# Norm sums as columns per block of tokens, and the norm of the renewed x by recursion, in a two-layer diffusion backbone

## The chip, the cores and the metric

The kernel runs on one core of one Trainium2 chip. The metric is the device time of one launch in microseconds. The kernel before takes 2223.82 us, the median of 3 runs (2221.72 to 2227.89).

## The reference, cut to what matters

384 tokens (128 of context, 256 latent) of width 1024 go through two layers, all in float32. Each layer has three sub-layers: a gated feed-forward net of width 2816, a token mixer (two kinds of attention and a recurrence, joined and projected by `w_out`), and a second feed-forward net. Each is wrapped alike:

```python
h = modulate(x, norm_pre, shift, scale)      # rmsnorm(x) * g * (1 + scale) + shift
y = sublayer(h)
x = x + gate * rmsnorm(y, norm_post)         # gate halved around the feed-forward nets
```

`rmsnorm` divides each token by the root of the mean of its 1024 squares plus 1e-6. `shift`, `scale` and `gate` come from a product of the conditioning vector with `ada_w`, one set for the context tokens and one for the latent ones. The outputs are x at the end and the new caches.

## The kernel before

x, y and h lie transposed: a tile k is 128 of the 1024 features on the partitions by 384 tokens along the row, eight tiles in all. Float32 products are made of three passes: a weight is split into `w_hi` (ScalarE, L1037) and `w_lo` (GpSimd, L534, two pieces of 128x512), h into `h_hi` and `h_lo`, and each k-tile of a unit takes three products per 128 columns (L597). A unit is up to four k-tiles by 256 columns, 24 products, and four units are in flight (`SPLIT`). The raw weights come through a ring of four buffers, in the order that SyncE issues. Phases follow one another: up0, down0, proj with the mixer, out, up1, down1. The phases down0, out and down1 make y, in four pairs of tiles. A pair is 22 k-tiles deep after the feed-forward nets (five units of four k-tiles and one of two) and 8 deep in out (two units).

Between a phase that makes y and the next one lies a gap; there are five. In a y phase, ScalarE squares each pair of y out of PSUM (`y_square`, L1134) and VectorE multiplies it by the gate factors `mG` into `y` (`y_out`, L1605) and adds the squares up in `y_sum`. In the gap TensorE sums over the partitions by products with a matrix of ones (`y_sums`, L700), so that the sum stands in all 128 partitions; ScalarE takes the root of the 128x384 sums (L1097), VectorE its reciprocal, and adds y times the root to x (`post`, L1566). Then the same for x: ScalarE squares it (L1119), TensorE sums (`x_sums`, L710), root, reciprocal, and `pre` (L1531) scales x into `sq`, from which ScalarE makes `h_hi` (L1126) and VectorE `h_lo` (`low`, L1524). The next phase starts by k-tiles (`by_tiles`, L667): two head units take k = 0 to 3 as each h tile comes, a third k = 4 to 7, and then the fourth, 96 products in all.

Products of the ada groups (`ada_unit`, L624; 8 units make one group of 1024 columns) fill the gaps: 22 units in four of them, 8 in layer 1's second. VectorE transposes and copies each group (`ada_take`, L1404). Every engine runs its own program in order, written out by hand, with semaphores between; a step on VectorE (L1395) waits for its own end before the next instruction.

## Time and profile before

| | |
|---|---|
| median of 3 runs | 2223.82 us |
| profiled execution | 2221.89 us |
| its span | 2220.1 us |
| TensorE busy | 2138.8 us (96%) |
| VectorE busy | 917.4 us (41%) |
| ScalarE busy | 903.5 us (41%) |
| GpSimd busy | 1241.3 us (56%) |
| DMA | 311.37 MB, mean 140 GB/s |

All times within the profile count from the span's start. PE is TensorE, PEld its weight loads, DVE VectorE, ACT ScalarE, POOL GpSimd, SP SyncE. A "q" behind an engine is its sequencer. Matmuls are pipelined: each is listed with its own duration, and the distance between starts is shorter. Of the shares, TensorE's is the one to follow; an engine at 41% can still be the one that all wait for inside a gap of 20 us.

### The profile page before, as it was taken

How to read it: one execution, taken by the hardware profiler on the slowest of the kernel's cores; microseconds unless marked ns; L12 is line 12 of the kernel's file. 1: busy time of each engine (PE TensorE's matmuls, PEld its weight loads, DVE VectorE, ACT ScalarE, POOL GpSimd, SP SyncE). 2: the span in 40 equal slices, each digit the busy share in tenths (PEclk: the TensorE clock that was granted, in tenths of full speed). 3: DMA queues.
4: the chain of work that ended last, by engine and by line, in shares of the span. 5: the costliest groups of instructions: out<-in, count | busy, mean ns of one | idle time of the engine just before them, and what ended most of it. 6: DMA issues, size and time to landing. Idle time of an engine off the chain costs nothing.

```text
span 2220.1 us, 32126 instructions
## 1 busy us (share of the span) xinstructions
PE 2138.8 (96%) x13212; PEld 2023.3 (91%) x13212; DVE 917.4 (41%) x1486; ACT 903.5 (41%) x1269; POOL 1241.3 (56%) x972
## 2 busy tenths in 40 slices
PE   6999999999898999999999999999999899899998
PEld 4999997988898988999979999799888899799997
DVE  5122116446766464121151221534576665622122
ACT  3222323256765534223243232324567646422332
POOL 2666654434478454666646665354435965366663
PEclk8999999999999999999999999999999999999999
DMA  7555674423232384445554446553322235244431
GB/s 283 150 174 171 226 260 149 126 86 88 72 89 87 112 286 124 124 143 168 194 178 124 147 125 226 194 152 88 87 78 77 86 114 172 70 139 124 124 124 66
DMA packets 306921, 311.37 MB, mean 140 GB/s; under 512 B 9923, under 2 KB 285655, under 8 KB 306775
## 3 DMA queue, kind: packets, MB, share of 16 engines
q1 hardware_dynamic: 299671, 303.55, 43.7%
q10 hardware_dynamic: 7104, 5.77, 0.8%
q8 instruction: 104, 1.70, 0.3%
q14 instruction: 42, 0.34, 0.0%
HBM read 305.35 MB, written 3.93 MB: 139 GB/s over the span
## 4 chain that ended last, share of the span: by engine, by line
PE 74%; DVE 12%; ACT 8%; POOL 3%; issue 2%; DMA 0%; SPq 0%; DVEq 0%; ACTq 0%
PE X L597 57%; PE S L597 6%; PE Ab L597 4%; POOL w_lo L534 1%; PE S L714 1%; ACT w_hi L1037 1%; POOL dec L562 1%; POOL dec L561 1%; PE X L775 1%; PE S L804 1%; ACT p L1190 1%; DVE mg_lo L1462 1%; PE X L857 1%; DVE gate_b L1473 1%; DVE root L1547 1%
## 5 line engine op out<-in xcount | busy, mean ns | idle before, releaser
L534 POOL TENSOR_TENSOR w_lo<-raw,w_hi 128x512 fp32r<-128x512 f32 (+1 forms) x872 | 1163.8, 1357 | 938.3 <-ACT w_hi L1037 928.8
L1037 ACT ACTIVATE w_hi<-raw 128x1024 fp32r<-128x1024 f32 (+1 forms) x436 | 453.1, 1041 | 716.4 <-PE X L597 678.1
L597 PE MATMUL X<-h_hi,w_hi 128*128 128x384 f32 x1600 | 538.1, 336 | 13.2 <-DVE h_lo L1527 13.2
L597 PE MATMUL X<-h_lo,w_hi 128*128 128x384 f32 x1600 | 536.3, 335 | 0.0
L597 PE MATMUL X<-h_hi,w_lo 128*128 128x384 f32 x1600 | 536.1, 335 | 0.0
L597 PEld LDWEIGHTS X<-h_hi,w_hi 128*128 128x128 f32 x1600 | 301.6, 189 | 21.0 <-DVE h_lo L1527 16.5
L597 PEld LDWEIGHTS X<-h_hi,w_lo 128*128 128x128 f32 x1600 | 301.8, 189 | 0.0
L597 PEld LDWEIGHTS X<-h_lo,w_hi 128*128 128x128 f32 x1600 | 301.7, 189 | 0.0
L1599 DVE TENSOR_TENSOR prod<-X,silu 128x768 f32<-128x768 f32 x44 | 42.1, 957 | 561.5 <-PE X L597 561.5
L597 PE MATMUL X<-act_hi,w_hi 128*128 128x384 f32 x704 | 235.7, 335 | 0.0
L597 PE MATMUL X<-act_hi,w_lo 128*128 128x384 f32 x704 | 235.2, 334 | 0.0
L597 PE MATMUL X<-act_lo,w_hi 128*128 128x384 f32 x704 | 235.2, 334 | 0.0
L1610 DVE TENSOR_SCALAR y<-X,mG 128x128 f32<-128x128 f32 x96 | 33.4, 411 | 337.7 <-ACT prod L1141 337.7
L597 PE MATMUL S<-h_hi,w_hi 128*128 128x384 f32 x480 | 166.3, 346 | 0.4 <-DVE proj L1441 0.4
L597 PE MATMUL S<-h_lo,w_hi 128*128 128x384 f32 x480 | 161.3, 336 | 0.0
L597 PE MATMUL S<-h_hi,w_lo 128*128 128x384 f32 x480 | 161.3, 336 | 0.0
L597 PEld LDWEIGHTS X<-act_hi,w_hi 128*128 128x128 f32 x704 | 132.1, 188 | 2.1 <-issue 2.1
L597 PEld LDWEIGHTS X<-act_lo,w_hi 128*128 128x128 f32 x704 | 132.2, 188 | 0.0
L597 PEld LDWEIGHTS X<-act_hi,w_lo 128*128 128x128 f32 x704 | 132.1, 188 | 0.0
L597 PE MATMUL Ab<-h_hi,w_hi 128*128 128x384 f32 x320 | 111.7, 349 | 0.7 <-DVE acc_e L1449 0.7
L597 PE MATMUL Ab<-h_hi,w_lo 128*128 128x384 f32 x320 | 107.2, 335 | 0.0
L597 PE MATMUL Ab<-h_lo,w_hi 128*128 128x384 f32 x320 | 107.2, 335 | 0.0
(364 smaller groups left out, 3074.8 us busy)
## 6 DMA issues: line engine op xcount, KB each, us to landing
raw<-in_w_in SPq DMA_DIRECT2D x124, 512.0 KB, 3.8
raw<-in_ffn_gate SPq DMA_DIRECT2D x88, 512.0 KB, 3.8
raw<-in_ffn_up SPq DMA_DIRECT2D x88, 512.0 KB, 3.8
raw<-in_ffn_down SPq DMA_DIRECT2D x80, 512.0 KB, 3.5
raw<-in_ada_w SPq DMA_DIRECT2D x48, 512.0 KB, 3.7
hold<-in_ada_w SPq DMA_DIRECT2D x29, 512.0 KB, 5.1
first_w<-in_ada_w SPq DMA_DIRECT2D x16, 512.0 KB, 10.5
hold_a<-in_ada_w SPq DMA_DIRECT2D x16, 512.0 KB, 6.3
```

Of the source, the lines that this page charges most:

```text
L534: ins = nc.gpsimd.tensor_tensor(slot(w_lo, u)[:, part], raw_of(u)[:, part], slot(w_hi, u)[:, part], SUB)
L561: nc.gpsimd.tensor_tensor(dst[:, :, 0:b], mid, src[:, :, 0:b], SUB)
L562: nc.gpsimd.tensor_tensor(dst[:, :, b:], src[:, :, b:], mid, SUB).then_inc(S["dec_ready"], 1)
L597: mm = nc.tensor.matmul(dst, w[:, k, m * 128:m * 128 + 128], r_, start=start and k + j == 0, stop=stop and k == u.nk - 1 and j == 2)
L714: mm = nc.tensor.matmul(S5[:, 0:T], ones, sq[:, k, :], start=k == 0, stop=k == KT - 1)
L775: mm = nc.tensor.matmul(X[n % 2][:, c, at_:at_ + k.shape[-1]], proj[64 * c:64 * c + 64, (AQ if kind == "a" else CQ) + h, b * 128:b * 128 + ...
L804: mm = nc.tensor.matmul((S5, S6)[c][:, 0:128], v, pT[:, c, j * 128:j * 128 + 128], start=j == 0, stop=j == len(kbs) - 1)
L857: mm = nc.tensor.matmul(X[0][:, j // 3, j % 3 * 128:j % 3 * 128 + 128], lev_k[n % 2][:, t], lev_q[n % 2][:, t], start=True, stop=True)
L1037: A(slot(w_hi, u), raw_of(u), ACT.Copy).then_inc(hi_ready[u.split], 1)
L1190: e = A(p[n % 2][:, c, 0:w], X[n % 2][:, c, 0:w], ACT.Exp, bias=nmax[:, n % 2, c:c + 1], accum_out=esum[:, n % 2, c:c + 1])
L1599: V.tensor_tensor(prod[:, :, :], X[1][:, :, 0:T], silu[:, :, :], MUL).then_inc(x_free[1], 1)
L1610: ins = V.tensor_scalar(y[:, 2 * i + m, t0:t1], X[u.dest][:, m, t0:t1], mG[:, 2 * i + m, g:g + 1], None, MUL)
```

## The change

The norm sums are made as columns: `token_sums` multiplies each block of 128 tokens (as the stationary side) with a column of `pick`, and gives sums of 128 tokens by 3 blocks. Roots and reciprocals are then 128x3, and `spread` turns a column of reciprocals into 128x384 in PSUM by three transposes of the broadcast column (banks S6 and S5, `SPREAD`).

The sum of squares of the renewed x is not taken from x. With g = y times the gate factors and r the inverse root of y, it is the old sum plus 2 r sum(x g) + r^2 sum(g g), kept in `x_sum` (VectorE, in `joint`). The products x g are added on VectorE and g g is squared on ScalarE, during the y phase. `post` and `pre` become one function, `joint`, which renews x three tiles ahead of the one that it scales.

In the y phases ScalarE does the gating of y out of PSUM (`gated`), beside the squares, tile by tile; the last pair is taken up when its first tile is whole (`half_done`). VectorE adds squares and products up. The last w_hi of a y phase moves into `gap`, behind these. Factors for the next norm (`factors`) are made at the first y unit of out rather than at the last. TensorE's `gap` has ada units 0, 1, 2 to 5 and 6 to 21 between the sums. The ada groups use two banks in place of three. In the last y phase only the squares are summed.

Of the diff, its core (the rest renames semaphores, moves small buffers and merges GpSimd's list of low parts into one call):

```diff
-    prod, o = at("prod", [128, 2, T], f32, o)
+    prod, o = at("prod", [128, 4, T], f32, o)
...
-        MOD = [Ab, S7, S6]
+        MOD = [Ab, S7]
+        SPREAD = (S6[:, 0:T], S5[:, 0:T])
...
+            def tokens(rows):
+                return [rows[:, b * 128:b * 128 + 128] for b in range(NB)]
+            def token_sums(dst, rows, start, stop):
+                for b, r in enumerate(tokens(rows)):
+                    mm = nc.tensor.matmul(dst[:, 0:NB], r, pick[:, NB - 1 - b:2 * NB - 1 - b], start=start and b == 0,
+                                          stop=stop and b == NB - 1)
+                return mm
+            def spread(dst, col):
+                for b in range(NB):
+                    mm = nc.tensor.transpose(dst[:, b * 128:b * 128 + 128], col[:, b:b + 1].broadcast_to([128, 128]), ident)
+                mm.then_inc(S["spread_ready"], 1)
+            def y_sums():
+                pe.wait_ge(S["y_sq_ready"], seen.next("y_sq_ready", KT))
+                token_sums(S5, prod[:, 2, :], True, False)
+                pe.wait_ge(S["parts_ready"], seen.next("parts_ready"))
+                token_sums(S5, silu[:, 0, :], False, True).then_inc(S["sum_ready"], 1)
             def gap(units):
+                ada_unit(units[0])
                 y_sums()
-                early = 12 if len(units) > 12 else len(units) // 2
-                for u in units[:early]:
+                pe.wait_ge(x_free[0], seen.value(("xf", 0)) + 1)
+                token_sums(X[0][:, 0, 0:NB], y_sum, True, False)
+                ada_unit(units[1])
+                pe.wait_ge(S["r_ready"], seen.next("r_ready"))
+                spread(SPREAD[0], r_t)
+                token_sums(X[0][:, 1, 0:NB], silu[:, 1, :], True, False)
+                pe.wait_ge(S["parts_ready"], seen.next("parts_ready"))
+                token_sums(X[0][:, 0, 0:NB], part, False, True)
+                pe.wait_ge(S["c_made"], seen.next("c_made", KT))
+                token_sums(X[0][:, 1, 0:NB], prod[:, 3, :], False, True).then_inc(S["cross_ready"], 1)
+                for u in units[2:6]:
                     ada_unit(u)
-                x_sums([])
-                for u in units[early:]:
+                pe.wait_ge(S["r_ready"], seen.next("r_ready"))
+                spread(SPREAD[1], r_t)
+                for u in units[6:]:
                     ada_unit(u)
                 return by_tiles
...
             def x_sums(units):
...
-                    mm = nc.tensor.matmul(S5[:, 0:T], ones, sq[:, k, :], start=k == 0, stop=k == KT - 1)
+                    mm = token_sums(S5, sq[:, k, :], k == 0, k == KT - 1)
...
-            def root_of_sums():
-                act.wait_ge(S["sum_ready"], seen.next("sum_ready"))
-                A(root[:, :], S5[:, 0:T], ACT.Sqrt, bias=eps[:, 0:1], scale=1.0 / D).then_inc(S["root_ready"], 1)
-            def gap(units):
-                root_of_sums()
-                act.wait_ge(S["ada_used"], units[2].n + 1)
-                x_squares(0, KT)
-                root_of_sums()
+            def root_of_sums(sums):
+                A(r_q[:, :], sums, ACT.Sqrt, bias=eps[:, 0:1], scale=1.0 / D).then_inc(S["root_ready"], 1)
+            def gap(units, upto):
+                highs(upto)
+                act.wait_ge(S["x_sum_made"], seen.next("x_sum_made"))
+                root_of_sums(x_sum[:, :])
...
-            def y_square(u):
-                n = seen.next("y_pairs")
-                if n > 1:
-                    act.wait_ge(S["y_added"], n - 1 - (n - 1) // 4)
-                    act.wait_ge(S["sum_ready"], seen.value("sum_ready"))
-                A(prod[:, :, :], X[u.dest][:, :, 0:T], ACT.Square).then_inc(S["y_sq_ready"], 1)
+            def y_squares(halves_done, cross):
+                def squared(u, k):
+                    if k >= 3:
+                        act.wait_ge(S["y_added"], seen.next("y_added"))
+                    A(prod[:, k % 2 * 2, :] if k else silu[:, 0, :], X[u.dest][:, k % 2, 0:T], ACT.Square).then_inc(S["y_sq_ready"], 1)
+                def gated(u, k):
+                    for g, (t0, t1) in enumerate(((0, SEQ), (SEQ, T))):
+                        ins = A(y[:, k, t0:t1], X[u.dest][:, k % 2, t0:t1], ACT.Identity, scale=mG[:, k, g:g + 1])
+                    ins.then_inc(S["g_made"], 1)
+                    seen.next("g_made")
+                def gated_squared(k):
+                    if cross:
+                        act.wait_ge(S["g_made"], KT * seen.value("y_phases") + k + 1)
+                        A(prod[:, k % 2 * 2 + 1, :] if k else silu[:, 1, :], y[:, k, :], ACT.Square).then_inc(S["c_made"], 1)
+                def go(u):
+                    i = u.tag[1]
+                    if i < 3:
+                        act.wait_ge(unit_done[u.split], u.split_turn + 1)
+                        if i == 0:
+                            act.wait_ge(S["mg_factor_made"], seen.next("mg_factor_made"))
+                        for k in (2 * i, 2 * i + 1):
+                            squared(u, k)
+                            gated(u, k)
+                        return
+                    act.wait_ge(S["half_done"], halves_done)
+                    squared(u, 6)
+                    gated(u, 6)
+                    gated_squared(6)
+                    act.wait_ge(unit_done[u.split], u.split_turn + 1)
+                    squared(u, 7)
+                    gated(u, 7)
+                    act.wait_ge(S["sum_ready"], seen.next("sum_ready"))
+                    root_of_sums(S5[:, 0:NB])
+                    gated_squared(7)
+                    seen.next("y_phases")
+                def behind(u):
+                    if u.tag[1] < 3:
+                        for k in (2 * u.tag[1], 2 * u.tag[1] + 1):
+                            gated_squared(k)
+                return go, behind
...
+            def inverse_root():
+                dve.wait_ge(S["root_ready"], seen.next("root_ready"))
+                V.reciprocal(r_t[:, :], r_q[:, :]).then_inc(S["r_ready"], 1)
+                dve.wait_ge(S["r_ready"], seen.next("r_ready"))
...
+            def joint(units):
+                def add_to_x(k):
+                    step(V.tensor_tensor(y[:, k, :], y[:, k, :], SPREAD[0], MUL))
+                    step(V.tensor_tensor(x[:, k, :], x[:, k, :], y[:, k, :], ADD))
+                inverse_root()
+                dve.wait_ge(S["spread_ready"], seen.next("spread_ready"))
+                add_to_x(0)
+                dve.wait_ge(S["cross_ready"], seen.next("cross_ready"))
+                step(V.tensor_tensor(grown[:, :], X[0][:, 1, 0:NB], r_t[:, :], MUL))
+                step(V.scalar_tensor_tensor(grown[:, :], X[0][:, 0, 0:NB], 2.0, grown[:, :], MUL, ADD))
+                step(V.tensor_tensor(grown[:, :], grown[:, :], r_t[:, :], MUL))
+                step(V.scalar_tensor_tensor(grown[:, :], x_sum[:, :], -1.0, grown[:, :], MUL, ALU.max))
+                V.tensor_tensor(x_sum[:, :], x_sum[:, :], grown[:, :], ADD).then_inc(S["x_sum_made"], 1)
+                step(V.tensor_tensor(y[:, 1, :], y[:, 1, :], SPREAD[0], MUL))
+                inverse_root()
+                step(V.tensor_tensor(x[:, 1, :], x[:, 1, :], y[:, 1, :], ADD))
+                add_to_x(2)
+                dve.wait_ge(S["spread_ready"], seen.next("spread_ready"))
+                dve.wait_ge(S["ada_used"], units[2].n + 1)
+                for k in range(KT):
+                    for g, (t0, t1) in GROUPS:
+                        ins = V.scalar_tensor_tensor(sq[:, k, t0:t1], x[:, k, t0:t1], mA[:, k, g:g + 1], SPREAD[1][:, t0:t1], MUL, MUL)
+                    ins.then_inc(S["norm_ready"], 1)
+                    if k == 1:
+                        ada_take(units[7])
+                    if k:
+                        low(k - 1)
+                    if k + 3 < KT:
+                        add_to_x(k + 3)
+                    dve.wait_ge(S["norm_ready"], seen.next("my_norm"))
+                low(KT - 1)
...
+            def y_out(cross):
+                def with_x(k):
+                    dve.wait_ge(S["g_made"], KT * seen.value("y_phases") + k + 1)
+                    if not cross:
+                        return
+                    if k == 0:
+                        V.tensor_tensor(y_sum[:, :], x[:, k, :], y[:, k, :], MUL)
+                    elif k < KT - 1:
+                        step(V.tensor_tensor(part[:, :], x[:, k, :], y[:, k, :], MUL))
+                        step(V.tensor_tensor(y_sum[:, :], y_sum[:, :], part[:, :], ADD))
                     else:
+                        V.tensor_tensor(part[:, :], x[:, k, :], y[:, k, :], MUL).then_inc(S["parts_ready"], 1)
+                def added(k):
+                    dve.wait_ge(S["c_made" if cross else "y_sq_ready"], KT * seen.value("y_phases") + k + 1)
+                    if k:
+                        n, at_ = 2 if cross else 1, k % 2 * 2
+                        step(V.tensor_tensor(silu[:, 0:n, :], silu[:, 0:n, :], prod[:, at_:at_ + n, :], ADD))
+                        dve.sem_inc(S["parts_ready" if k == 6 else "y_added"], 1)
+                def freed(u):
+                    dve.wait_ge(S["g_made"], KT * seen.value("y_phases") + 2 * u.tag[1] + 2)
+                    dve.sem_inc(x_free[u.dest], 1)
+                    seen.next(("mine", u.dest))
                 def go(u, i):
-                    dve.wait_ge(S["y_sq_ready"], seen.next("y_sq_ready"))
-                    for m in range(2):
-                        for g, (t0, t1) in GROUPS:
-                            ins = V.tensor_scalar(y[:, 2 * i + m, t0:t1], X[u.dest][:, m, t0:t1], mG[:, 2 * i + m, g:g + 1],
-                                                  None, MUL)
-                    ins.then_inc(x_free[u.dest], 1)
-                    dve.wait_ge(x_free[u.dest], seen.next(("mine", u.dest)))
-                    if i == 0:
-                        V.tensor_tensor(y_sum[:, :], prod[:, 0, :], prod[:, 1, :], ADD).then_inc(S["y_added"], 1)
-                    elif i < 3:
-                        step(V.tensor_tensor(y_sum[:, :], y_sum[:, :], prod[:, 0, :], ADD))
-                        V.tensor_tensor(y_sum[:, :], y_sum[:, :], prod[:, 1, :], ADD).then_inc(S["y_added"], 1)
                     if i < 3:
-                        dve.wait_ge(S["y_added"], seen.next("y_added"))
+                        freed(u)
+                        for k in (2 * i, 2 * i + 1):
+                            with_x(k)
+                        for k in (2 * i, 2 * i + 1):
+                            added(k)
+                        return
+                    with_x(6)
+                    added(6)
+                    with_x(7)
+                    freed(u)
+                    seen.next("y_phases")
                 return go
```

## Rows read from the trace of the kernel before

**Rows 1.** The chain of waits: start us, us, engine, what it writes, line, count.

```profile
337.34 2.56 DVE root L1569
...
346.42 3.03 PE S L714 x8
...
350.09 2.56 DVE root L1547
...
355.04 29.39 PE X L597 x168
```

**Rows 2.** Timeline of ScalarE, first gap: start us, us, operation, out<-in, count [idle before].

```profile
332.18 1.06 ACT L1037 ACTIVATE w_hi<-raw 128x1024 fp32r<-128x1024 f32 x1 [3.10 <-PE X L597]
...
334.20 0.81 ACT L1141 ACTIVATE prod<-X 128x768 f32<-128x768 f32 x1 [0.96 <-PE X L597]
```

**Rows 3.** Timeline of VectorE, first gap.

```profile
339.93 0.96 DVE L1572 TENSOR_TENSOR y<-y,root 128x768 f32<-128x768 f32 x1
...
340.99 0.96 DVE L1574 TENSOR_TENSOR x<-x,y 128x768 f32<-128x768 f32 x1
...
354.24 0.75 DVE L1527 SCALAR_TENSOR_TENSOR h_lo<-sq,mB,h_hi 128x128 fp32r<-128x128 f32 x2
...
354.90 0.55 DVE L1541 TENSOR_TENSOR sq<-y,root 128x384 f32<-128x384 f32 x1
```

**Rows 4.** Timeline of TensorE, first gap.

```profile
336.55 1.50 PE L636 MATMUL S<-hold_sq,c_col 128*32 128x256 f32 x24
...
341.32 0.61 PE L636 MATMUL Ab<-hold_b,c_col 128*32 128x256 f32 x8
```

**Rows 5.** Timeline of GpSimd, first gap.

```profile
333.32 2.51 POOL L534 TENSOR_TENSOR w_lo<-raw,w_hi 128x512 fp32r<-128x512 f32 x2 [1.62 <-ACT w_hi L1037]
```

**Rows 6.** Timeline of VectorE, layer 0's out phase.

```profile
808.99 1.53 DVE L1618 TENSOR_TENSOR y_sum<-y_sum,prod 128x384 f32<-128x384 f32 x1
...
819.29 1.15 DVE L1495 TENSOR_SCALAR mA<-mA 128x16 f32<-128x16 f32 x1
```

**Rows 7.** VectorE's groups by shape: count | busy us, mean ns | idle before.

```profile
L1470 DVE TENSOR_TENSOR gate_b<-S,gate_b 128x384 f32<-128x384 f32 x12 | 6.6, 547 | 4.2 <-ACT gate_b L1078 4.2
...
L1408 DVE STREAM_TRANSPOSE ada_t<-S 128x256 f32<-128x256 f32 x12 | 5.3, 442 | 8.5 <-PE S L636 8.5
...
L1593 DVE RECIPROCAL r_tok<-S 128x3 f32<-128x3 f32 x1 | 0.2, 174 | 0.0
```

**Rows 8.** ScalarE's groups by shape.

```profile
L1126 ACT ACTIVATE h_hi<-sq,mB 128x256 fp32r<-128x256 f32 x48 | 23.7, 494 | 0.0
...
L1126 ACT ACTIVATE h_hi<-sq,mB 128x128 fp32r<-128x128 f32 x48 | 19.1, 398 | 43.0 <-DVE sq L1541 34.7 <-DVEq L1519 8.4
...
L1074 ACT ACTIVATE gates<-S 128x384 f32<-128x384 f32 x22 | 10.6, 481 | 8.2 <-PE S L597 8.2
...
L1304 ACT ACTIVATE dend<-ends 128x4 f32<-128x4 f32 x4 | 0.6, 188 | 0.0
```

**Rows 9.** Timeline of TensorE, end of the kernel.

```profile
2206.62 0.52 PE L1010 MATMUL S<-con,root 128*128 128x128 f32 x3 [0.76 <-ACT root L1097]
```

**Rows 10.** Timeline of TensorE, layer 1's second gap.

```profile
1914.47 6.90 PE L714 MATMUL S<-sq,con 128*128 128x384 f32 x16 [4.14 <-ACT sq L1119]
```

**Rows 11.** Windows: us, busy PE, PEld, DVE, ACT, POOL, then granted clock, DMA, GB/s.

```profile
1915.00:1918.00 3.00, 3.00 (x7) 1.55 (x6) 2.90 (x4) 1.24 (x3) 0.00 (x0) 0.59 0.00 0
...
1927.00:1930.00 3.00, 3.00 (x11) 3.00 (x12) 3.00 (x10) 1.60 (x4) 0.00 (x0) 0.62 0.00 0
```

**Rows 12.** Timelines of TensorE and VectorE, start of the kernel.

```profile
35.42 1.08 PE L636 MATMUL S<-first_w,c_col 128*32 128x256 f32 x8 [0.23 <-DMA first_w<-in_ada_w]
...
38.65 0.43 DVE L1408 STREAM_TRANSPOSE ada_t<-S 128x256 f32<-128x256 f32 x1
```

**Rows 13.** Timelines of ScalarE and VectorE, end of the kernel.

```profile
2203.44 0.81 ACT L1141 ACTIVATE prod<-X 128x768 f32<-128x768 f32 x1 [13.87 <-PE X L597]
...
2206.58 0.96 DVE L1585 TENSOR_TENSOR x<-x,root 128x768 f32<-128x768 f32 x1 [0.81 <-ACT root L1097]
```

190 lines of the change are left out of this document (79 added, 111 removed).

## The prediction

> **What bounds the kernel now.** The page first: TensorE is busy 96% of the 2220.1 us span. Then the chain of waits, in order of time. It is TensorE's weight products, 0.175 us each (29.39 us for 168), broken at the same place five times: between the last product of a phase that makes y and the first of the next. There it runs through ScalarE's root, VectorE's reciprocal, x, the sums of x squared, a second root and a second reciprocal [rows 1]. I call the end of y's last product T0; in the first such gap ScalarE's square starts there, at 334.20 [rows 2], so T0 = 334.16. The next product starts at 355.04, T0+20.9. From there TensorE runs without a stop through the 96 products of the four head units (16.8 us), to T0+37.7. The other four look alike in this view. Everything outside them is bound by products, which the change leaves alone, so I price the five gaps, the start and the end, and ask whether the new work in the y phases reaches back into TensorE.
>
> **What goes.** Two reciprocals of 128x384, 2.56 us each [rows 1], become 128x3, 0.17 us [rows 7]: 4.8 us a gap. The squares of x, their eight sums (the last four 3.03 us [rows 1]) and the second long root leave the chain. TensorE's 22 ada units stay: 12 take (341.93 - 336.55)/12 = 0.45 us each [rows 4].
>
> **What comes, after a down phase (three gaps).** Times are from T0.
> ScalarE. The last unit has two k-tiles, so tile 6 is whole six products early, at -1.04. ScalarE has just ended a w_hi (332.18 + 1.06 is -0.92 [rows 2]). Then, in order: square 6 (0.48, nearest row a 128x384 read of PSUM [rows 8]), gate 6 (0.40 + 0.49, overlapped as a pair in 0.80), its square 0.5, square 7, gate 7: g_made(7) is there at +0.4, the last square at +1.4, the last gate at +2.2.
> VectorE. x6*y6 and its addition to y_sum (0.55 each free), then silu += prod, 128x768 (0.96 [rows 3]). GpSimd's w_lo pair runs from 333.32 to 335.83 [rows 5], to +1.7. How a VectorE operation with both inputs in SBUF fares beside it: the same addition takes 1.53 us [rows 6], and a 128x16 step takes 1.15, where one of 128x3 alone takes 0.17 [rows 7]: it lasts until the w_lo piece of 1.27 us ends. So x6*y6 ends at +2.1, y_sum at +2.7, silu at +3.65. (If it slips in ahead of the piece, 1.1 less.)
> Then the path: three column products and one root of 128x3 (0.45 by three transposes at 0.52 [rows 9], 0.2 by a small ScalarE operation [rows 8]), reciprocal 0.17: +4.7. Spread by three transposes, 0.52: +5.3. y0 and x0, 0.55 + 0.55 with a semaphore each (a step costs its duration and 0.06 to 0.1: 339.93 to 340.99 [rows 3]): +6.5. The cross sums come beside this, at +6.3. Five small steps of the recursion at 0.2: +7.5 if free. But ScalarE's last w_hi now stands in the gap, behind the square of y7, and lets GpSimd go at about +6.0 to +8.6. Three of the five steps read only SBUF and I let them wait for both pieces: +8.95. Root, reciprocal: +9.7; meanwhile y1. Then x1 and x2: +11.5.
> The loop over k: two STT against the spread root 0.65, two STT for h_lo 0.66 (354.24 to 354.90 [rows 3]), y and x of k+3 1.2 for five of the eight: 2.55 us a k. Sum: 8 x 0.65 + 8 x 0.66 + 5 x 1.2 + one ada_take in VectorE's queue at k=1 (0.44 [rows 7] + 0.17 + waits, 0.75) + 0.75 of waits = 18.0. h(0) is ready at +15.6, h(4) at +25.9, h(7) at +29.5.
> TensorE. Ada units 6 to 15 from +10.3, 4.4 us; with two banks in place of three, unit 16 waits until VectorE has copied the first group at k=1 (+14.7); the products start at +17.3. That isn't last for long: a k costs TensorE 12 x 0.175 = 2.1 and VectorE 2.55, so VectorE has it back by k=4, and the end is h(7) + six products + head[3]'s 24: 29.5 + 1.05 + 4.2 = +34.8. Before: +37.7. Gain 2.9 a gap. Between T0 and h(7) VectorE barely gets earlier (before, it ended near +29.9); what is gained is that TensorE's products now lie inside VectorE's loop instead of behind it.
> GpSimd and SP: the w_hi moved past costs head[3] some 3 us of a wait that has 20 to spare, and the ring's loads follow it. After the loop ScalarE's first w_hi comes at +28.5; GpSimd is through at +31, 3.8 us ahead of the need.
>
> **After the out phase (two gaps).** Its y blocks last 8.4 us (two units of 24 products) instead of 24. Per block VectorE gets four 128x384 and two 128x768 operations with both inputs in SBUF, GpSimd has four w_lo pieces. Beside each other these exclude one another: 4 x 0.42 + 2 x 0.83 + 4 x 1.27 = 8.4 us, all of the block, and VectorE may start only 2.6 us into it, after both gates. Alternating one for one, I get block 0 done 7.5 after y0, block 1 at 19.7, block 2 at 29.8, that is at T0+4.8. ScalarE's square of tile 7 waits for that (its buffer). So the first reciprocal is at about +8.0 instead of +4.7, and the end at +38.1: 0.4 slower than before. Bounds: never blocked, the root comes 2 us earlier than in a down gap, end +32.8 (5 faster); each piece also with the 0.3 us by which it stretches, end +40.5 (3 slower). I take 0.4 since the row of 1.53 us [rows 6] is from this very phase. In layer 1 the clock already falls there: granted 0.59 of full speed in 1915 to 1918, and 0.62 in 1927 to 1930, as the products start [rows 11], which alone costs 3 x 0.38 = 1.1 us; after the change a slow stretch at the start of the products lies under VectorE's loop, so this gap gives 1.
>
> In the down phases the same VectorE and ScalarE work has 24 us a block: hidden, and w_lo has about 12 us of lead (three units of 4.2).
>
> **Start.** The 2.55 us reciprocal goes before the first h, but the last ada unit's products end at 36.50 and VectorE's transpose of them started at 38.65 [rows 12]: at most 2.1 us, which I take. **End.** Today from the last square (2203.44) 3.1 us to the first x*root at 2206.58 [rows 13]. After: square 6, gate, square 7, gate to +1.7, sums beside, root 0.2, spread 0.52: +2.6, and no reciprocal between the chunks (0.3): 0.9 less.
>
> **Sum.** -3 x 2.9 + 0.4 - 1.0 - 2.1 - 0.9 = -12.3. The profiled execution took 2221.89 us (span 2220.1 + 1.8) and is 1.9 under the median, 2223.82. 2221.9 - 12.3 = 2209.6; the loop over k has many waits that I priced at nothing or 0.06, so I round up to 2211.
>
> One place where rule and row can part: the Trainium skill (SBUF — State Buffer, "SBUF: two separate sides") says that VectorE and GpSimd share one port pair as a lock held for a whole instruction, and that VectorE wants it with two SBUF inputs or in a two-port mode; an operation with one input in PSUM would then be free. The trace agrees where it can: a product with one PSUM input has a mean of 0.547 us amid GpSimd's work [rows 7]. By the rule alone both STT of the loop and y*spread are safe at any time; were they held like the others, nothing changes in the loop, since GpSimd is idle there.
>
> **Rivals.**
> A. The locks are not met: GpSimd's pieces fall beside VectorE's instead of on them. For it: which of two comes first is a matter of tenths, and my tenths are sums of many terms. Against: I see the 1.5 us of [rows 6] in every block of both y phases. Each down gap then ends by +32.6, the out gaps at +32.8: -3 x 5.1 - 4.9 - 6.3 - 3 = -29.5, 2193. Half of it, the out phase still lagging, 2202.
> B. It does what it says and pays nothing: VectorE's loop is the bound, and 0.3 more per k (a PSUM operand, semaphores) is 2.4 a gap, eating the 2.9; with the out gaps at +3 each the sum is -1.5 + 6 - 3 = +1.5: 2223.
> C. Slower: TensorE's clock. After T0 it now waits 3.2 us (down) or 6.6 us (out) with one ada unit done, and then does crumbs. In layer 1's second gap it idled 4.14 us [rows 10], and the grant then fell to the level of 1.2 GHz (a mean of 0.59 over three us [rows 11]). If it falls in each gap and holds through the ada run, 16 units cost 0.43 more each, 6.9; the products start at +24, lose 1.7 more in a slow stretch (1.5 times the 1.1 of rows 11), and end at +42.6: +4.9 three times, +8 in layer 0's out gap: 22.7 - 1 - 3 = +18.7, 2240. It decides once the products start later than +20.9. Against: a mean of 0.59 is a fall that hardly outlasts the three us, and 3.4 us at half speed ahead of +17.3 is 1.7 us, which VectorE's loop covers. The Trainium skill (TensorE: Matmul & The Clock Gate, "HAM oscillation — how this bites in real kernels") warns of this pattern, bursts behind waits that each start cold; the trace agrees for that one gap.
>
> **Chances.** The forecast 0.48 (own range 2204 to 2217), A and its half 0.23, B 0.18, C 0.11. The range for 8 in 10: A's half and some of A below, B above: 2199 to 2223. A measurement tells 0.3%, 6.7 us, from no change. Faster by more (under 2217.1): the forecast nearly whole, A, a little of B: 0.74. Same: 0.16. Slower (C, and B's worst): 0.10.
>
> **What would show it.** Reciprocals of 0.17 us; x6*y6 over 1 us beside a w_lo piece; in a down gap the first root near +4.4, the first product near +17, TensorE waiting on h_lo by some 0.4 us a k from k=4; in the out gap the first root near +7.7 and additions of 1.5 to 2.2 us; granted clock 1.0 in the down gaps. Wrong: the products start after +21, or the steps of VectorE's loop cost over 2.9 us, or x_free holds TensorE inside a y phase.

## The result, and the profile after

The changed kernel takes 2234.99 us, the median of 6 runs (2232.56 to 2238.86), against 2224.1 for the kernel before in the same session (6 runs): ratio 1.005, 95% interval 1.0037 to 1.0063. It is slower, where 2211 was forecast. All times compared here and below are of the fast state; the one exception, among e10's twelve executions, took 4847.52 us, and e10's median is 2221.71 with it and 2221.3 without. The profiled execution took 2232.56 us with a span of 2230.7, 10.6 over the span before. TensorE's mean granted clock over the span is 0.976 (before 0.990); its busy time grew from 2138.8 to 2154.8 us, though the sums of 384 columns are gone.

I read the after profile gap by gap, since everything between is the same. T0 is again the end of y's last product. In brackets, the same distance before.

| gap | first product of next phase | end of the 96 head products | forecast end |
|---|---|---|---|
| layer 0, down0 | +23.3 (20.9) | +40.3 (37.8) | +34.8 |
| layer 0, out | +25.4 (20.9) | +42.3 (37.8) | +38.1 |
| layer 0, down1 | +23.6 (20.9) | +40.5 (37.8) | +34.8 |
| layer 1, down0 | +22.1 (20.9) | +39.0 (37.8) | +34.8 |
| layer 1, out | +22.5 (21.0) | +42.1 (39.5) | +38.5 |

The five ends lose 2.5 + 4.5 + 2.7 + 1.2 + 2.6 = 13.5 us. The start gives 2.0 by the first gap (its T0 is 332.16, before 334.16), the end of the kernel 0.4, a stretch between gaps 0.5: 10.6. The 2.0 at the start is no safe gain: in e1 to e4 and e8 below, which leave all that stands ahead of it as in the changed kernel, the first T0 lies at 334.9 to 338.1, later than before.

TensorE in the first gap, from the timeline of the kernel after (start us, us, engine, line, operation, out<-in, count, idle before). It stands where [rows 4] stood:

```profile
333.25 0.83 PE L700 MATMUL S<-pick,prod 128*128 128x3 f32 x6 [0.52 <-ACT prod L1173]
335.66 1.44 PE L700 MATMUL S<-pick,silu 128*128 128x3 f32 x6 [1.58 <-DVEq L1705]
336.96 1.42 PE L700 MATMUL X<-pick,y_sum 128*128 128x3 f32 x6
...
339.32 0.90 PE L707 MATMUL S<-con,r_t 128*128 128x128 f32 x3
...
344.64 2.79 PE L638 MATMUL S<-hold,c_col 128*32 128x256 f32 x24
```

Three float32 column products are six instructions, and take 0.83 us, not 0.45. From the second sum on the same six take 1.44, three transposes 0.90 where [rows 9] had 0.52, and 24 ada products 2.79 where [rows 4] had 1.50. The windows of this stretch say why (us, busy of PE, PEld, DVE, ACT, POOL, then granted clock, DMA, GB/s):

```profile
332.00:334.00 2.00, 1.48 (x15) 0.90 (x14) 1.57 (x2) 1.79 (x5) 2.00 (x2) 1.00 1.00 358
334.00:336.00 2.00, 0.42 (x3) 0.34 (x2) 1.82 (x3) 0.00 (x0) 0.14 (x1) 0.78 0.85 295
336.00:338.00 2.00, 2.00 (x11) 2.00 (x11) 0.43 (x2) 0.86 (x3) 0.00 (x0) 0.50 0.63 238
...
344.00:346.00 2.00, 2.00 (x24) 0.87 (x20) 1.79 (x8) 0.30 (x1) 0.00 (x0) 0.50 0.13 53
...
348.00:350.00 2.00, 2.00 (x32) 1.00 (x34) 1.60 (x4) 0.00 (x0) 0.00 (x0) 0.81 0.01 4
350.00:352.00 2.00, 2.00 (x44) 1.14 (x40) 1.90 (x7) 1.60 (x4) 0.00 (x0) 1.00 0.03 8
```

TensorE waits 0.52 and 1.58 us around one sum, the grant falls to 0.50 (1.2 GHz), and stays there for 13.6 us by these shares (335.1 to 348.8), although from 335.66 on TensorE is busy without a break. The chain of waits confirms that the path now runs through these small products (start us, us, engine, what it writes, line, count); before, it ran through two long reciprocals [rows 1]:

```profile
335.66 1.44 PE S L700 x6
337.10 1.28 PE X L700 x6
338.38 1.01 PE S L638 x8
339.39 0.83 PE S L707 x3
340.23 3.63 PE X L700 x18
343.86 3.57 PE S L638 x32
```

VectorE in the same gap, where [rows 3] stood:

```profile
332.40 0.61 DVE L1694 TENSOR_TENSOR part<-x,y 128x384 f32<-128x384 f32 x1 [12.53 <-ACT y L1178]
333.05 1.51 DVE L1695 TENSOR_TENSOR y_sum<-y_sum,part 128x384 f32<-128x384 f32 x1
...
337.43 0.18 DVE L1584 RECIPROCAL r_t<-r_q 128x3 f32<-128x3 f32 x1 [1.18 <-ACT r_q L1129]
...
343.97 0.16 DVE L1634 TENSOR_TENSOR grown<-X,r_t 128x3 f32<-128x3 f32 x1 [2.23 <-PE X L700]
...
348.37 0.74 DVE L1649 SCALAR_TENSOR_TENSOR sq<-x,mA,S 128x128 f32<-128x128 f32 x2 [1.00 <-PE S L707]
```

The work that the change meant to shorten is short: 0.18 and 0.16 us. But VectorE waits before nearly each of these for TensorE's sums or spreads, or for a root made of such a sum.

Layer 0's out phase, VectorE, where [rows 6] stood. Beside w_lo an addition of 128x384 takes 1.54 us and one of 128x768 1.93, so the first reciprocal is done at T0+7.8:

```profile
818.41 1.54 DVE L1694 TENSOR_TENSOR part<-x,y 128x384 f32<-128x384 f32 x1
...
821.55 3.86 DVE L1704 TENSOR_TENSOR silu<-silu,prod 128x768 f32<-128x768 f32 x2
...
829.66 0.18 DVE L1584 RECIPROCAL r_t<-r_q 128x3 f32<-128x3 f32 x1 [1.18 <-ACT r_q L1129]
```

The start, TensorE and then VectorE, where [rows 12] stood. The column products of two tiles of x squared (x12) take 1.91 us and then 2.72, since the clock falls here too:

```profile
20.17 1.91 PE L700 MATMUL S<-pick,sq 128*128 128x3 f32 x12
...
23.03 2.72 PE L700 MATMUL S<-pick,sq 128*128 128x3 f32 x12
...
35.10 0.64 PE L638 MATMUL S<-first_w,c_col 128*32 128x256 f32 x8 [0.66 <-DMA first_w<-in_ada_w]
```

```profile
35.81 0.45 DVE L1480 STREAM_TRANSPOSE ada_t<-S 128x256 f32<-128x256 f32 x1 [0.83 <-PE S L638]
```

### The profile page after: what moved, and what is told of

Same layout as the page of the kernel before. It is cut to its first block, busy times and chain, and to the rows that moved or that the text cites. A ratio compares the mean times of both kernels' runs of the same rounds, so it can differ in the third digit from the quotient of the medians.

```text
span 2230.7 us, 32592 instructions
## 1 busy us (share of the span) xinstructions
PE 2154.8 (97%) x13353; PEld 2052.5 (92%) x13353; DVE 937.3 (42%) x1489; ACT 929.3 (42%) x1389; POOL 1260.3 (56%) x972
## 4 chain that ended last, share of the span: by engine, by line
PE 73%; DVE 11%; ACT 8%; POOL 4%; issue 2%; SPq 1%; DMA 1%; ACTq 0%; DVEq 0%
PE X L599 54%; PE S L599 6%; PE Ab L599 4%; POOL w_lo L539 2%; PE S L638 2%; PE Ab L638 1%; ACT w_hi L1068 1%; PE X L700 1%; DVE silu L1704 1%; POOL dec L567 1%; POOL dec L566 1%; PE X L808 1%; PE S L837 1%; ACT p L1263 1%; DVE mg_lo L1538 1%
## 5 line engine op out<-in xcount | busy, mean ns | idle before, releaser
L539 POOL TENSOR_TENSOR w_lo<-raw,w_hi 128x512 fp32r<-128x512 f32 (+1 forms) x872 | 1182.8, 1380 | 930.3 <-ACT w_hi L1068 923.0
L1678 DVE TENSOR_TENSOR prod<-X,silu 128x768 f32<-128x768 f32 x44 | 42.1, 958 | 555.1 <-PE X L599 555.1
L1263 ACT ACTIVATE p<-X,nmax 128x384 f32<-128x384 f32 (+1 forms) x96 | 48.1, 506 | 114.9 <-DVE nmax L1757 114.8
```

The costliest lines, as they stand in the source:

```text
L539: ins = nc.gpsimd.tensor_tensor(slot(w_lo, u)[:, part], raw_of(u)[:, part], slot(w_hi, u)[:, part], SUB)
L1263: e = A(p[n % 2][:, c, 0:w], X[n % 2][:, c, 0:w], ACT.Exp, bias=nmax[:, n % 2, c:c + 1], accum_out=esum[:, n % 2, c:c + 1])
L1678: V.tensor_tensor(prod[:, 0:2, :], X[1][:, :, 0:T], silu[:, :, :], MUL).then_inc(x_free[1], 1)
```

## The experiments

The theory after the result: TensorE's clock (T1). A wait starts the fall, the column products behind it keep the clock down, and everything on the path through TensorE takes up to twice as long. Rivals: the count of small products and weight loads costs the time at any clock (T2); VectorE's lag behind GpSimd after out (T3); the work queued ahead of the first spread.

**e1** puts idle products ahead of y's sums, so that TensorE does not wait.

```diff
                 ada_unit(units[0])
+                pe.wait_ge(x_free[0], seen.value(("xf", 0)) + 1)
+                for _ in range(22 if any(units is PHASES[l, "gap1"] for l in range(DEPTH)) else 10):
+                    nc.tensor.matmul(X[0][:, 1, 128:512], ones, con[:, 0:384], start=True, stop=True)
                 y_sums()
...
```

> The changed kernel with idle products put into TensorE's wait after T0: 10 products of ones by 384 constant columns (22 after out), into columns of a PSUM bank that nobody reads. They do no useful work. Theory 1 (the clock): the grant no longer falls at T0+3, the column sums take 0.7 us each instead of 1.3 and the ada units 0.43 instead of 0.86, the next phase starts near T0+17.5 instead of +23.3 to +25.4, and the kernel takes 2205 to 2212. If the column sums with their 3 columns cannot hold the clock, it falls later and the start is near +20: 2218 to 2224. Theory 2 (the number of small products and loads is the cost, the clock only goes with it): nothing moves but the order, 2232 to 2238.

Measured: 2246.7 us (ratio to before 1.0103, 1.0086 to 1.012). An idle product cost 0.67 us, two instructions, so ten took 6.7 us and delayed the sums. As a timing it missed (2205 to 2212 was forecast). But the clock stayed at 1.00 through the first and fourth gap, and 24 ada products took 1.48 us again; in the second and third it fell all the same, though later and for half as long. TensorE in e1's first gap:

```profile
335.39 6.72 PE L722 MATMUL X<-con 128*128 128x384 f32 x20
...
347.35 1.48 PE L638 MATMUL S<-hold,c_col 128*32 128x256 f32 x24
```

**e2** runs six ada units ahead of y's sums, and none between them.

```diff
-                ada_unit(units[0])
+                for u in units[:6]:
+                    ada_unit(u)
                 y_sums()
...
-                ada_unit(units[1])
...
-                for u in units[2:6]:
-                    ada_unit(u)
```

> The changed kernel with ada units 0 to 5 all ahead of the sums of y (instead of unit 0 there, unit 1 behind the y_sum sums and 2 to 5 behind the cross sums). Theory 1 (the clock): 2.6 us of the 3.2 us wait of a down gap are filled, the grant holds there, start near +17, minus 5.5 us in three gaps; in the out gaps 4 us of wait stay and the clock falls: minus 2 there. 2212 to 2218. Theory 2 (no clock): only the 1.8 to 3.6 us of ada units ahead of the second spread leave the path, but the same ada work has to be done before the next phase, so the start moves by the 2 us of wait that it now fills: 2225 to 2229.

Measured: 2222.6 us (0.9996, 0.9987 to 1.0006), 12 us under the changed kernel by an order alone, and between the two forecasts (T1 2212 to 2218, T2 2225 to 2229), so it decides nothing. Products start at +19.0, +23.0, +20.7, +19.0, +19.4, and the clock still falls in every gap.

**e3** puts the first spread directly behind y's sums (the work in front of it was a rival).

```diff
+                pe.wait_ge(S["r_ready"], seen.next("r_ready"))
+                spread(SPREAD[0], r_t)
                 token_sums(X[0][:, 0, 0:NB], y_sum, True, False)
                 ada_unit(units[1])
-                pe.wait_ge(S["r_ready"], seen.next("r_ready"))
-                spread(SPREAD[0], r_t)
```

> The changed kernel with the first spread ahead of the y_sum sums and ada unit 1 in TensorE's queue. Theory 1 and 2: the same products stand in the same wait and the start is set by the end of the ada units, so x0 comes 1.7 us earlier and nothing else moves: 2232 to 2237. Rival (the queue in front of the spread is what costs, VectorE's path decides): minus 2 us a gap, 2223 to 2227.

Measured: 2240.06 us (1.0073, 1.0058 to 1.0088), no gain; as the cause of this loss, that rival falls (it asked for 2223 to 2227). The first spread is done at T0+6.5 in place of +8.1, and the 96 products end at +40.8, no earlier. TensorE now waits for the reciprocal instead, and its sums still take 1.44:

```profile
340.37 1.44 PE L700 MATMUL S<-pick,silu 128*128 128x3 f32 x6 [1.57 <-DVEq L1704]
342.47 0.87 PE L707 MATMUL S<-con,r_t 128*128 128x128 f32 x3 [0.66 <-DVE r_t L1583]
```

**e4** is e2 with two more ada units ahead of the second spread.

```diff
-                ada_unit(units[0])
+                for u in units[:6]:
+                    ada_unit(u)
                 y_sums()
...
-                ada_unit(units[1])
...
-                for u in units[2:6]:
+                for u in units[6:8]:
...
```

> As the run with ada units 0 to 5 first, and units 6 and 7 between the cross sums and the second spread, so that TensorE does not wait there. Theory 1 (the clock): as that run or 1 us a gap better in the down gaps, 2209 to 2217. Theory 2: the wait of about 1.7 us for the second root is filled, 5 x 1 to 1.7 us less than that run.

Measured: 2217.36 us (0.9972, 0.9962 to 0.9981), faster than the kernel before and 5.2 us under e2, which T2's forecast for this step (5 x 1 to 1.7) fits as well as T1's range. TensorE in its first gap:

```profile
343.12 0.81 PE L700 MATMUL X<-pick,silu 128*128 128x3 f32 x6
343.79 1.42 PE L700 MATMUL X<-pick,part 128*128 128x3 f32 x6
```

TensorE has gone on here from 337.77 with no wait over a few hundredths of a us. The clock, 1.00 to that point, falls in the middle of a run of column products, and the next six take 1.42 us. So a wait isn't needed for the fall. That would leave it to what TensorE does, which the next run tests alone.

**e5** leaves the order of the changed kernel and makes each column product move 128 columns of `pick` (the further ones are zeros, their results are not read).

```diff
-    pick, o = at("pick", [128, 2 * NB - 1], f32, o)
+    pick, o = at("pick", [128, NB - 1 + 128], f32, o)
...
-                    mm = nc.tensor.matmul(dst[:, 0:NB], r, pick[:, NB - 1 - b:2 * NB - 1 - b], start=start and b == 0,
+                    mm = nc.tensor.matmul(dst, r, pick[:, NB - 1 - b:NB - 1 - b + 128], start=start and b == 0,
...
```

> The changed kernel, but each of the 18 column products of a gap moves 128 columns instead of 3 (the table with the single column of ones is 130 wide, the other 125 columns are zeros and are not read). Products, weight loads, order and waits are the same. Theory 1 (it is the clock: products of 3 columns keep TensorE busy by the trace, but the granted clock falls to 0.50 under them): granted clock stays near 1.00 from the second sum on in the first gap, a sum of three takes about 0.8 us there instead of 1.28, an ada unit 0.45 instead of 0.88, products start at +19.5 to +21 after y's last product in the four gaps after down (now +22.1 to +23.6), the kernel takes about 2223 us (2218 to 2228), 0.5% less than the changed kernel. Rival 2 (the count of small products and weight loads alone costs the time): the gap is as long or longer, products at +23.5 to +25, 2236 to 2242 us.

Measured: 2214.3 us (0.9962, 0.995 to 0.9974): 20.7 us less than the changed kernel (19.6 by the two ratios to the kernel before), by columns that nobody reads. It is more than T1 asked for (2218 to 2228), and T2 falls: the products and loads are as many. TensorE, then the windows, in e5's first gap (T0 333.82):

```profile
337.32 0.93 PE L700 MATMUL S<-pick,silu 128*128 128x128 f32 x6 [1.47 <-DVEq L1705]
338.09 0.83 PE L700 MATMUL X<-pick,y_sum 128*128 128x128 f32 x6
...
342.36 1.48 PE L638 MATMUL S<-hold,c_col 128*32 128x256 f32 x24
```

```profile
336.00:338.00 2.00, 0.68 (x6) 0.68 (x7) 1.73 (x3) 0.00 (x0) 0.00 (x0) 1.00 0.82 225
338.00:340.00 2.00, 2.00 (x22) 1.47 (x21) 0.17 (x1) 1.62 (x3) 0.01 (x1) 1.00 0.35 141
...
344.00:346.00 2.00, 2.00 (x35) 1.23 (x39) 1.90 (x5) 0.00 (x0) 0.00 (x0) 1.00 0.68 238
```

The wait is still there (1.47 us), the clock is not lost. Products start at +17.7, +20.8, +19.1, +17.7, +20.3. In the second and third gap it still fell, to a mean of 0.55 to 0.6 over 4 us, and was back behind that; in the fifth it was low for some 7 us, and again as the products started.

**e6** is e4 with the 128-column table. (Its expectation puts the first spread directly behind y's sums; in the code of e4 and e6 the sums of `y_sum` stand between.)

> The kernel of e4 (six ada units before the first sums, two before the second spread, the first spread directly behind y's sums) with the 128-column table of e5. Theory 1: the granted clock, which in e4 fell to 0.50 from 343.8 in the first gap, stays at 1.00 up to the products of the next phase; start of the products at +16.5 to +17.5 after down (e4 18.1) and +18 to +20 after out (e4 20.46 and 18.86); 2212 us (2208 to 2216). Rival 2: wider products only make it longer, 2218 to 2222 us.

Measured: 2212.35 us (0.995, 0.9938 to 0.9963), the lowest of those that compute everything, and faster than both kernels. Starts: +17.7, +20.0, +17.7, +17.7, +18.2. The clock held at 1.00 up to the next products in four of the five gaps; in layer 1's second it fell at +14.8, while TensorE waited for h. After down the start is no better than e5's best: there VectorE's chain sets the end.

**e7** is e6 without VectorE's products x times gated y in the out phases.

```diff
+                    if short:
+                        if k == 0:
+                            step(V.memset(y_sum[:, :], 0.0))
+                        if k == KT - 1:
+                            V.memset(part[:, :], 0.0).then_inc(S["parts_ready"], 1)
+                        return
```

> e6 with VectorE's products x times gated y, and their running sum, left out of the two out phases (y_sum and the last part are set to zero instead, so the recursion's sum of x is wrong there): it prices what VectorE still adds behind GpSimd's lock on the shared port in these phases. Rival 3 (the lag of VectorE in the out phases is a main part of the loss): gap after out as short as after down, start at +16.5 to +17.5 in place of about +19.5 in layer 0, and y's last product of the phase up to 2 us earlier, together 5 to 8 us less than e6, about 2205 us. Theory 1 holds the lag for a smaller part, 1 to 4 us less than e6.

Measured: 2207.23 us (0.9925, 0.9912 to 0.9939), 5.1 under e6. The gap after out in layer 0 shrank from +20.0 to +17.5 (end +34.8), and y's last product came no earlier. In layer 1 the end moved from +37.3 to +35.1. T3 is real, and worth 5 us over both out phases, a quarter of what e5 won; my forecast had it in.

**e8** is e1 with 5 and 9 idle products.

> The changed kernel with idle products of 384 columns ahead of y's sums as in e1, but 5 instead of 10 after down and 9 instead of 22 after out, so that at 0.67 us each they fill only the time in which TensorE waits anyway. Theory 1: clock held at 1.00 in the gap, sums 0.67 us apart, ada units 0.43; products start at +19.5 to +20.5 after down and +22 to +24 after out, 2224 us (2220 to 2230). Rival 2 (the count of small products): as the changed kernel or worse, +23 to +25, 2235 to 2242 us.

Measured: 2222.73 us (0.9998, 0.9989 to 1.0007). The time is as T1 forecast, but by luck: the clock was not held. The first gap (T0 338.12) holds the clearest picture of the fall. TensorE, then the windows:

```profile
345.48 0.81 PE L700 MATMUL X<-pick,part 128*128 128x3 f32 x6
346.15 1.40 PE L700 MATMUL X<-pick,prod 128*128 128x3 f32 x6
...
348.34 2.79 PE L638 MATMUL S<-hold,c_col 128*32 128x256 f32 x24
```

```profile
342.00:344.00 2.00, 2.00 (x23) 1.98 (x25) 0.38 (x2) 0.62 (x3) 0.00 (x0) 1.00 0.56 217
346.00:348.00 2.00, 2.00 (x17) 1.76 (x20) 1.06 (x3) 0.00 (x0) 1.89 (x2) 0.55 0.00 0
350.00:352.00 2.00, 2.00 (x19) 0.82 (x15) 1.02 (x2) 0.00 (x0) 0.00 (x0) 0.50 0.39 158
```

TensorE is busy in every window, and drops to half speed. In the third gap of the same run the same instructions, again without a wait, kept the clock at 1.00, and the products start at +18.5 in place of +21.3:

```profile
1133.23 0.81 PE L700 MATMUL X<-pick,prod 128*128 128x3 f32 x6
```

So the clock can fall during 3-column products without a wait, and does not always.

**e9** reorders e5: on VectorE the squares' sums of tiles 4 to 6 before their products with x; on TensorE three ada units first, the first spread at once, the sums of `y_sum` behind it, and five ada units ahead of the second spread.

```diff
-                        for k in (2 * i, 2 * i + 1):
-                            with_x(k)
-                        for k in (2 * i, 2 * i + 1):
-                            added(k)
+                        for do in (added, with_x) if i == 2 else (with_x, added):
+                            for k in (2 * i, 2 * i + 1):
+                                do(k)
...
+                    added(6)
                     with_x(6)
-                    added(6)
```

> The kernel of e5 with the order changed at y's end: VectorE adds the squares of tiles 4, 5 and 6 before it makes their products with x (so the sum of y's squares is complete before the last products), TensorE runs three ada units first instead of one, the first spread stands directly behind y's sums, and the products of y_sum stand behind it; five ada units between the recursion's sums and the second spread. From e5's and e6's rows: the add of tile 6 began 2.2 us (336.25 against 334.06) behind the product with x that stood before it, so the first reciprocal comes 1.0 to 1.6 us earlier after down and about 1.3 us earlier after out; products start at +16.3 to +17 after down (e5 17.7, 17.7 and 19.1) and +18 to +19 after out (e5 20.75 and 20.25). Theory: 2208 us (2205 to 2212). Rival: the gap is set by VectorE's total work from y's last tile to the fifth h_lo (the same in any order), and the time stays at e6's 2212 us.

Measured: 2213.6 us (0.9957, 0.9944 to 0.997); the rival stands nearer. After down the start is +17.1 three times, 0.6 under e5's best and less than forecast, because the add that now comes first meets the w_lo piece in the product's stead, as e9's VectorE row shows:

```profile
334.37 1.69 DVE L1703 TENSOR_TENSOR silu<-silu,prod 128x768 f32<-128x768 f32 x1 [12.07 <-ACT prod L1185]
```

After out (+21.6, +20.2) it won nothing: e5 had +20.8 and +20.3.

**e10** is e9 with the last w_hi behind the second root.

```diff
-                highs(upto)
                 act.wait_ge(S["x_sum_made"], seen.next("x_sum_made"))
                 root_of_sums(x_sum[:, :])
+                highs(upto)
```

> e9 with ScalarE's last copy into w_hi moved behind the root of x's sums, so that GpSimd's two w_lo pieces (2.8 us) lie beside VectorE's loop instead of beside the recursion (in e5 they lay at 339.99 to 342.81 and the add to x took 1.00 us in place of 0.56). Theory of the shared port: what the recursion wins (0.6 to 1.5 us: one add of 1.60 against 0.56 and one step of 0.72 against 0.16 in e6) the loop loses in equal part, within 1 us of e9 either way. Rival: the recursion's path ends earlier and the loop has room, 3 to 5 us less than e9 over five gaps; or the head's w_lo comes too late and products wait, 3 us or more over e9.

Measured: 2221.71 us (0.9994, 0.9985 to 1.0003), 8 more than e9. The recursion did run free, but the raw buffer came free later, and TensorE's ada unit waits for its load, a wait that e9 does not have (and it waits 0.86 us for VectorE's copy of the ada group, for 0.25 in e9):

```profile
350.39 0.64 PE L638 MATMUL S<-raw,c_col 128*32 128x256 f32 x8 [0.97 <-DMA raw<-in_ada_w]
```

The products start at +18.9 there, for +17.1 in e9. These are the waits I can show; whether they account for all 8 us stays open.

**e11** is e9 with six ada units first after out.

> e9 with six ada units ahead of y's sums after the two out phases (e9 has three; after down three stay), and two in place of five ahead of the second spread there. In e9 the granted clock fell in these gaps while TensorE waited for the squares' sum (the wait of 3.25 us ahead of 1902.04; then 1.28 us for a sum of three, 1.49 in the row), in e6 with its six units it did not (0.67 between sums). Theory 1 (clock): cross sums end 1.3 to 1.6 us earlier after out, start of the products +19 to +20.3 in layer 0 (e9 21.58) and +18 to +19 in layer 1 (e9 20.16), the other gaps unchanged at +17.1; 2210.5 us (2208 to 2213). Rival: VectorE's products with x decide these gaps alone, 2213 to 2214 us as e9.

Measured: 2213.22 us (0.9952, 0.994 to 0.9964), as e9. The expected gain in layer 0 did not come: TensorE still waited 1.97 us for the squares' sum, the clock fell to 0.50 from about 829, and the cross sums took 1.28 each, up to 835.4; start +22.9. In layer 1 part of it came: +19.5, for +18 to +19 forecast and +20.2 in e9.

**e12** is e5 with 3 columns at the start and 128 in the gaps and at the end.

> The kernel of e5 with the 128-column table in the gaps (and at the end) only; the 24 column products of x's squares at the start move 3 columns as in the changed kernel. It tells where the 20 us between the changed kernel and e5 lie. Theory 1: in the gaps alone, since the start waits for the last ada weights there (products from 38.57 in the changed kernel, 39.39 in e5); the clock falls at about 21 us of the start as in the changed kernel, and the whole takes 2213.5 us (2211 to 2217). Rival: the fall of the clock at the start costs later work too (weights and splits of the first phase), 2220 us or more.

Measured: 2217.58 us (0.9968, 0.9957 to 0.9979), just above T1's 2211 to 2217 and under the rival's 2220; its interval and e5's overlap. So most of the 20 us lie in the gaps, and the 3.3 us between the two runs stay open. In its first gap, where e5 kept the clock, the wait of 1.47 us was followed by a fall, but TensorE was back at 1.00 in the window 340 to 342, where the changed kernel's windows read 1.00 only from 350:

```profile
336.00:338.00 2.00, 2.00 (x16) 1.78 (x19) 0.48 (x2) 1.31 (x3) 0.00 (x0) 0.63 0.55 219
338.00:340.00 2.00, 2.00 (x14) 1.19 (x13) 0.11 (x1) 0.30 (x1) 1.62 (x2) 0.52 0.00 0
340.00:342.00 2.00, 2.00 (x21) 1.88 (x24) 1.25 (x2) 0.00 (x0) 0.87 (x1) 1.00 0.11 16
```

**The five gaps side by side.** For each profiled execution: the first T0, the five stretches from T0 to the end of the 96 products added up, and the mean granted clock in them.

| run | first T0, us | five gaps, us | clock |
|---|---|---|---|
| before | 334.2 | 190.6 | 0.98 |
| after | 332.2 | 204.2 | 0.83 |
| e1 | 334.9 | 215.5 | 0.96 |
| e2 | 338.0 | 187.8 | 0.86 |
| e3 | 336.9 | 207.2 | 0.82 |
| e4 | 337.8 | 183.2 | 0.87 |
| e5 | 333.8 | 183.7 | 0.95 |
| e6 | 335.6 | 179.6 | 0.98 |
| e7 | 332.4 | 174.9 | 0.97 |
| e8 | 338.1 | 192.3 | 0.92 |
| e9 | 333.6 | 181.3 | 0.95 |
| e10 | 333.8 | 190.3 | 0.94 |
| e11 | 334.4 | 181.8 | 0.95 |
| e12 | 332.2 | 185.4 | 0.94 |

Of e5's 20.7 us the gaps give 20.5, and 18.8 of them are there in e12, so the gain is in the gaps. And e4, with 3 columns and a clock that falls in every gap, has gaps as short as e5's; I read this as the order of its work: six ada units fill the wait, so fewer stand on the path where the clock is low. Either edit wins back the loss; both together (e6) win only 4 us more. The first T0 differs by 6 us among executions, so a run that is 3 us apart from another in its median, as e4 from e5, need not be so in its gaps.

## Why the prediction was wrong

The forecast was −12.3 us, the profiled result +10.6. Of the difference of 22.9, 22.8 lies in the five gaps. Times of the first gap from T0, for the kernel after and for e5, the same program but for the 128 columns, and in this gap at full clock:

| step | forecast | after | e5 |
|---|---|---|---|
| x6*y6, y_sum, silu done | +3.65 | +3.4 | +3.4 |
| first reciprocal done | +4.7 | +5.45 | +4.9 |
| first spread done | +5.3 | +8.1 | +6.15 |
| cross sums ready | +6.3 | +11.7 | +8.15 |
| x_sum | +8.95 | +12.8 | +9.4 |
| second spread done | +10.3 | +16.1 | +10.7 |
| loop over k begins | +11.5 | +16.2 | +11.9 |
| one k | 2.55 | 2.49 | 2.50 |
| products start | +17.3 | +23.3 | +17.7 |
| end of 96 products | +34.8 | +40.3 | +35.0 |

**The step that failed** is the one under rival C: "a mean of 0.59 is a fall that hardly outlasts the three us, and 3.4 us at half speed ahead of +17.3 is 1.7 us, which VectorE's loop covers". I had the wait, the fall and its price for ada units, and took the length of the fall from a gap where TensorE went on with 384-column products [rows 10, 11]. In the changed kernel it goes on with 3-column products, and the fall lasts 13.6 us, the last 5 of them with ada units and a spread, behind the last column product. Nor did it lie under VectorE's loop: the sums and spreads stand ahead of the loop, so their doubling moves it as a whole, by 4.7 us (+16.2 for +11.5; +11.9 in e5). The ada units behind them then doubled too. With the clock held (e5) the first gap ends at +35.0 against my +34.8. Rival C had it nearly: products from +24 and 2240 us, for +22 to +25 and 2235. It got 0.11. The Trainium skill (TensorE: Matmul & The Clock Gate, "HAM oscillation — how this bites in real kernels") tells of bursts that start cold behind waits. The after trace agrees in kind for the first fall, with shorter waits (0.52 and 1.58 us) than the section's; e4 and e8 show a fall without any wait, which that section's pattern would not give.

**Column sums mis-sized.** "Three column products 0.45 us" came from three transposes. Each float32 product here is two instructions, each with its weight load: 0.83 us for three at full clock, 0.67 from sum to sum. On the path ahead of x_sum five such sums stand behind the first: cross sums at +8.15 in e5, not +6.3. Since I let the recursion wait for GpSimd until +8.95 anyway, little of it came through (x_sum +9.4). The queue ahead of the first spread (y_sum's sum and an ada unit) was left out: the spread is done 1.2 us behind the reciprocal in e5 and 2.6 in the changed kernel, for a forecast of 0.6.

**VectorE and GpSimd's lock.** Right in size (1.51 us beside w_lo in both), wrong in place: it hit y_sum's addition and not x6*y6, with the same sum. The grown steps ran free in the changed kernel, since the slow clock had brought them behind w_lo; in e6 one of them took 0.73.

**After out.** First reciprocal forecast at about +8.0, measured at +7.8; the end forecast at +38.1, measured +42.3 in the changed kernel and +38.0 in e5. The lag was predicted well, the clock was not: the grant is at 0.50 from about 827 to 840. In layer 1, +38.5 forecast, +42.1 after and +39.4 in e5; the 1.0 us of gain I gave it was an error by itself, since the clock falls again as the products start.

**Loop, start, end.** A k costs 2.49 (forecast 2.55), and the loop is the bound at full clock, as said. Start: forecast −2.1, at the first product −2.8 (38.57 for 41.40), at the first T0 −2.0. That agreement may be luck: with the same start the first product comes at 38.8 to 42.9 in e1 to e4 and e8, and the first T0 at 334.9 to 338.1. The clock falls at the start as well, at about 21 us during x's column sums, where before it held until about 30, and TensorE seems to have room for that, for it waits for the last ada weights at 35.10 anyway. End: forecast −0.9, measured −0.4 (the first x times root at T0+3.1 for a forecast of +2.6; six instructions per sum again). VectorE at the end, where [rows 13] stood:

```profile
2216.82 0.18 DVE L1663 RECIPROCAL r_tok<-r_q 128x3 f32<-128x3 f32 x1 [1.65 <-ACT r_q L1129]
2217.48 0.95 DVE L1668 TENSOR_TENSOR x<-x,S 128x768 f32<-128x768 f32 x1 [0.49 <-PE S L707]
```

**Rivals.** A (locks not met) did not happen. B (pays nothing) doesn't hold: e5 and e6 gain 0.4% and 0.5%, so the idea of the change pays once the clock is kept (and 0.3% in e4, where it isn't). C was the case.

What stays open: why the clock was not lost in e5's first gap and fell for 3 to 4 us in the same gap of e12, though the instructions and waits of that gap are alike; the same between e5's first and third gap, and between e8's first and third. With the order unchanged, wider column products shorten the time at low clock on the whole (a mean of 0.95 over the gaps for 0.83); what decides in which gap it falls, the runs do not show.

## What to carry to other kernels

When a change puts small TensorE work on the path, look up the granted clock of each stretch where such work runs today, and price everything on the path at 1.2 GHz until something shows that it stays at 2.4. A fall prices not the wait but all that follows until the clock is back, and what TensorE does then bears on how long that is. Here columns that nobody reads bought 20 us, and moving ready work into the wait, ahead of the small products (e4), bought 17.6. Where moved columns are free in time, they are the smaller edit; try them first.

## What the runs showed of the hardware

- A float32 product that moves 3 columns costs the same as one of 128: from sum to sum 0.67 us for three in e1 (3 columns, 342.53 to 343.20) and 0.67 in e5 (128 columns, 339.80 to 340.47), both at full clock. Both are six instructions and six weight loads.
- TensorE can be 100% busy in the profile's windows and still be granted 0.50: from 336 to 348 us in the changed kernel, and from 346 us in e8 with no wait for 8 us before. The busy time of these windows does not show it; the granted clock does.
- The same wait of 1.47 us was followed by no fall (e5, first gap; e12, third) or by some 3.5 us of low clock (e5, third; e12, first), with the same instructions behind it.
- An addition of 128x768 on VectorE beside w_lo takes 1.93 us (3.86 for two, changed kernel, 821.55), free 0.96.
